# Pair loop of a hybrid RWKV-7 layer: the first inversion level made per direction, one PE item and the adaLN products moved

## The reference, cut to what matters

```
def step(S, inp):
    r_t, w_t, k_t, v_t, kk_t, b_t = inp
    sa = einsum('bhij,bhj->bhi', S, kk_t)
    S = S * w_t[:, :, None, :] - sa[..., None] * b_t[:, :, None, :] \
        + v_t[..., None] * k_t[:, :, None, :]
    return S, einsum('bhij,bhj->bhi', S, r_t)
# per direction d: first over the context, then over the latents from that state
mod = silu(c) @ w_mod + b_mod      # adaLN rows; (2048,) @ (2048, 12288)
```

## Time and profile before

| | |
|---|---|
| median of 3 runs | 2997.85 us (2994.82 to 2999.31) |
| the profiled execution's own time | 2995.07 us |
| its span in the profile | 2993.1 us |
| PE busy | 2841.4 us (95%) |
| DVE busy | 1839.5 us (61%) |
| ACT, POOL busy | 1002.5 us (33%), 579.6 us (19%) |
| mean DMA rate | 138 GB/s |
| mean granted TensorE clock | 0.979 |

### The profile page before, as it was taken

One profiled execution on the slowest core, in us unless ns is written; L12 is line 12 of the kernel. 1 busy time (PEld: TensorE's weight loads), 2 busy tenths in 40 slices (PEclk: granted clock), 3 DMA queues, 4 the chain that ended last, 5 costly groups with the idle time before them and its releaser, 6 DMA issues.

```text
span 2993.1 us, 70020 instructions
## 1 busy us (share of the span) xinstructions
PE 2841.4 (95%) x27808; PEld 2207.5 (74%) x27808; DVE 1839.5 (61%) x3324; ACT 1002.5 (33%) x1715; POOL 579.6 (19%) x708
## 2 busy tenths in 40 slices
PE   5899999999999999999989999999989999999997
PEld 1246665566656566666556699999979999999997
DVE  1115666677666767666675544444378888885434
ACT  1123322333322333332231433333354444443333
POOL 0003222333122233222231110000013333330000
PEclk9799999999999999999999999999989999999998
DMA  8621332222332222233214545554525555554553
GB/s 323 268 77 63 107 107 93 70 74 89 103 107 93 82 75 86 93 106 107 79 53 148 204 148 182 186 182 170 198 99 183 182 182 182 182 182 156 182 174 134
DMA packets 75291, 412.28 MB, mean 138 GB/s; under 512 B 9200, under 2 KB 11888, under 8 KB 42736
## 3 DMA queue, kind: packets, MB, share of 16 engines
q1 hardware_dynamic: 74352, 407.51, 39.5%
q0 software_dynamic: 768, 2.10, 0.2%
HBM read 405.38 MB, written 4.19 MB: 137 GB/s over the span
## 4 chain that ended last, share of the span: by engine, by line
PE 84%; DVE 8%; issue 3%; DMA 3%; ACT 1%; SPq 0%; DVEq 0%; ACTq 0%; PEldq 0%
PE PB L671 18%; PE Q L919 6%; PE Q L920 6%; PE Q L924 6%; PE PB L919 4%; PE PB L920 4%; PE PB L924 4%; PE CH L924 3%; PE CH L920 3%; PE CH L919 3%; DMA ring<-w_mod_dram 3%; PE Q L808 3%; PE PB L656 2%; PE Q L794 2%; PE Q L815 2%
## 5 line engine op out<-in xcount | busy, mean ns | idle before, releaser
L671 PE MATMUL PB<-hT,ring 128*128 128x512 f32 (+1 forms) x1536 | 673.5, 552 | 6.4 <-PEq L660 5.4
L1615 DVE TENSOR_TENSOR w_lo_r<-ring,w_hi_r 128x1536 fp32r<-128x1536 f32 (+3 forms) x178 | 386.9, 2174 | 269.8 <-ACT w_hi_r L1217 269.8
L1217 ACT ACTIVATE w_hi_r<-ring 128x2048 fp32r<-128x2048 f32 (+2 forms) x178 | 325.8, 1831 | 453.7 <-PE Q L924 211.3
L671 PEld LDWEIGHTS PB<-hT,ring 128*128 128x128 f32 x1536 | 256.8, 189 | 120.9 <-issue 70.7
L920 PE MATMUL PB<-hT_r,w_hi_r 128*128 128x256 f32 x832 | 204.6, 285 | 0.0
L1475 DVE SCALAR_TENSOR_TENSOR arena<-ring,csilp,arena 128x512 f32<-128x512 f32 x240 | 193.5, 806 | 5.2 <-DMA ring<-w_mod_dram 1.0
L1775 DVE TENSOR_TENSOR w_lo_r<-ring,w_hi_r 128x1408 fp32r<-128x1408 f32 x62 | 101.2, 1633 | 147.9 <-ACT w_hi_r L1331 147.9
L1876 POOL TENSOR_TENSOR w_lo_r<-ring,w_hi_r 128x512 fp32r<-128x512 f32 x88 | 118.4, 1346 | 361.4 <-ACT w_hi_r L1217 361.4
L919 PE MATMUL PB<-hT_r,w_hi_r 128*128 128x256 f32 x704 | 175.7, 289 | 4.7 <-DVE hT_r L1702 4.7
L919 PE MATMUL Q<-ff_hi_r,w_hi_r 128*128 128x256 f32 x704 | 175.6, 288 | 1.8 <-ACT w_hi_r L1331 1.8
L920 PE MATMUL Q<-ff_lo_r,w_hi_r 128*128 128x256 f32 x704 | 172.9, 284 | 0.0
(11 more groups left out here) (266 smaller groups left out, 6096.5 us busy)
## 6 DMA issues: line engine op xcount, KB each, us to landing
ring<-w_up_dram SPq DMA_DIRECT2D x88, 1024.0 KB, 4.8
ring<-w_mod_dram SPq DMA_DIRECT2D x128, 512.0 KB, 3.7
ring<-w_rkv_dram SPq DMA_DIRECT2D x48, 1024.0 KB, 5.8
ring<-w_down_dram SPq DMA_DIRECT2D x64, 704.0 KB, 4.0
ring<-w_mod_dram SPq DMA_DIRECT2D x32, 1024.0 KB, 7.8
ring<-w_ga_dram SPq DMA_DIRECT2D x16, 1024.0 KB, 4.8
ring<-w_gb_dram SPq DMA_DIRECT2D x16, 1024.0 KB, 4.8
ring<-w_pa_dram SPq DMA_DIRECT2D x16, 1024.0 KB, 4.8
```

The lines of the kernel that those rows point to most:

```text
L671: last = mm(PB[slot % 2][:, 0:cols], tile(n, kt), hT[:, kt, 0:cols], start=(kt == 0), stop=(kt == KT - 1))
L1217: f(w_hi_r[:, r % 2, 0:n], ring[:, r, 0:n], ACT.Copy).then_inc(hi_rdy, 1)
L1615: tt(w_lo_r[:, r, 0:n], ring[:, r, 0:n], as_f32(w_hi_r[:, r % 2, 0:n]), ALU.subtract).then_inc(lo_rdy, 1)
```

## The change

Four edits inside the pair loop:

- DVE makes the first level per direction: after the scores of d come TU (two operations of 64x256) and ZU (128x256) of d, and after NL of d come TL and ZL of d. Five operations of 512 columns become ten of 256. The signals `zu_rdy` and `zl_rdy` are still given once, behind d = 1.
- PE's first item (W0) goes ahead of the five waits that stand before the levels.
- The products move back: k = 0 to level 4, none in scan step 0, two in steps 1 to 6 (k = 2s-1, 2s), k = 13 in step 7, k = 14 and 15 behind the sum of the readout. Before, step s had k = 2s and 2s+1 and only k = 15 stood behind the sum.
- BODY_STEPS, the count of DVE's own semaphore steps in a pair, goes from 38 to 41.

```diff
@@ PE, body
+                if more >= 1:
+                    between(i + 1, 0)
+                else:
+                    behind_last(0)
                 pe.wait_ge(xt_sb, i * 4 + 4)
                 pe.wait_ge(nl_sb, i * 2 + 2)
                 pe.wait_ge(bonv_rdy, i + 1)
...
                 for lv in range(LEVELS - 1):
                     b = 2 << lv
-                    if lv == 0:
-                        if more >= 1:
-                            between(i + 1, 0)
-                        else:
-                            behind_last(0)
                     pe.wait_ge(zu_rdy, i * LEVELS + lv + 1)
@@ DVE, body, in the loop over d
+                    dve.wait_ge(sc_sb, i * 4 + 2 * d + 2)
+                    for h in range(2):
+                        hr = slice(64 - 64 * h, 128 - 64 * h)
+                        m = V.tick(tt(single(TU[hr], 1 - d), single(SC[d][h][hr, :, 0], 1 - d),
+                                      single(wide(off_mask[:, 0, 0, :], NCH)[hr], 1 - d), ALU.mult))
+                    V.need(m)
+                    z = tt(single(ZU[d], 1 - d), single(wide(eye2[:, :], NCH), 1 - d), single(TU, 1 - d), ALU.subtract)
                     if d == 1:
-                        dve.wait_ge(sc_sb, i * 4 + 4)
-                        for h in range(2):
-                            hr = slice(64 - 64 * h, 128 - 64 * h)
-                            m = V.tick(tt(by_chunk(plain(TU[hr], 1)), woven(SC2[h][hr, :, :, 0], 1),
-                                          plain(wide(off_mask[:, 0, 0, :], NCH)[hr], 1), ALU.mult))
-                        V.need(m)
-                        tt(by_chunk(woven(ZU2, 1)), plain(wide(eye2[:, :], NCH), 1), by_chunk(plain(TU, 1)), ALU.subtract).then_inc(zu_rdy, 1)
+                        z.then_inc(zu_rdy, 1)
                     dve.wait_ge(nl_ps, i * 2 + d + 1)
                     tt(NL[d], chunks(Q[0][:, :]), wide(score_mask[:, 1 - d, 0:C], NCH), ALU.mult).then_inc(nl_sb, 1)
-                dve.wait_ge(nl_sb, i * 2 + 2)
-                flow(tt(by_chunk(plain(TL, 1)), by_chunk(woven(NL2, 1)), plain(wide(off_mask[:, 0, 0, :], NCH), 1), ALU.mult))
-                tt(by_chunk(woven(ZL2, 1)), plain(wide(eye2[:, :], NCH), 1), by_chunk(plain(TL, 1)),
-                   ALU.subtract).then_inc(zl_rdy, 1)
+                    dve.wait_ge(nl_sb, i * 2 + d + 1)
+                    flow(tt(single(TL, d), single(NL[d], d), single(wide(off_mask[:, 0, 0, :], NCH), d), ALU.mult))
+                    z = tt(single(ZL[d], d), single(wide(eye2[:, :], NCH), d), single(TL, d), ALU.subtract)
+                    if d == 1:
+                        z.then_inc(zl_rdy, 1)
@@ DVE, levels
                         for n in range(2 * lv + (lv == 0), 2 * lv + 2):
                             inputs(i + 1, n)
+                        if lv == LEVELS - 2:
+                            mod_product(i, 0)
@@ DVE, scan
                     if more >= 1:
-                        for k in range(2 * s, min(2 * s + 2, 15)):
+                        for k in range(max(2 * s - 1, 1), min(2 * s + 1, 14)):
                             mod_product(i, k)
...
                 tt(ra, yd[0], yd[1], ALU.add).then_inc(ysum_rdy, 1)
                 if more >= 1:
+                    mod_product(i, 14)
                     mod_product(i, 15)
```

More of the change, by code:

```diff
@@ L34 @@
 QUAD = P // 4
-BODY_STEPS = 38
+BODY_STEPS = 41
 ARENA = 32100
@@ L448, in plain, with single @@
             return bass.AP(v.tensor, v.offset, walk([part] + chunk, col, b, b))
+        def single(v, odd):
+            return v.rearrange("p c (n two) -> p c n two", two=2)[:, :, :, odd]
         def by_chunk(v):
```

## The result

The changed kernel takes 2962.61 us in the median of 4 runs (2958.76 to 2965.55), the kernel before 2998.44 (2994.82 to 2999.31) beside it. The profiled execution took 2960.52 us, 34.55 less than that of before; the prediction's sum had 28.8.

The account below looks back on a forecast made before the run. PE bounds the kernel, waiting 41.6 us, mostly behind a late DVE. Levels 16.5, scan 13.6, pair 14 1.5, readout -2.8 sum to 28.8 us off: 2969 us against 2997.85, range 2958 to 2987.

Parts of the forecast that it names:

- What bounds: Pair loop: PE is busy nearly always; its waits in four totals, 41.6 us, are the most the change can give.
- Levels, 1.10 a pair: Start of the levels: half operations at 0.42 to 0.55 us close PE's gaps of 0.60 and 0.51; 16.5 us in 15 pairs.
- rival 4: Levels: the shift is swallowed by something seen as hidden, POOL's copy or a bank held by ACT; 2977 us, chance 0.13.
- The item: Start of the levels: W0, no longer waiting for NL, starts at 709.61, which saves 0.60 us.
- Level 4, 0.25: Product k = 0 waits for a POOL operation, so the last ZU update starts 0.25 us late; bounds 0 and 1.5.
- Scan, 0.97 a pair: Scan step 1: waits of 0.42 and 0.90 go, less 0.25 for level 4 and 0.1 left; 13.6 us in 14 pairs.
- Rival 1: Scan step 1: all of the 0.90 stays because the L1545s meet POOL operations; 2982 us, or 2988; chance 0.17.
- Pair 14 and the ends: Pair 14, with no second projection beside its scan, waits more; 1.5 us taken for it.
- Readout, 0.2: Two products behind the sum make L1571 0.3 us late; PE loses 0.2 a pair, -2.8 us in 14 pairs.
- Loads, nothing: Half loads in the scan: issue to need falls to 4.4 us against a median landing of 3.7; hidden, 0.7 to spare.
- Rival 2: Levels: half operations cost like whole ones, 4 us slower, 3002 us; chance 0.05.

Follow-up runs that it names:

- the table early: The changed kernel with ACT loading the tanh table ahead of its wait for the projections, not ahead of W0's tanh: 2958.61 us, ratio 0.9872.
- the experiment: The changed kernel with each half load (2 to 7) asked for one product later, computation the same: 2984.12 us, ratio 0.9952.

## Why the prediction was right, and where it was off

- **What bounds.** Right: four waits of PE behind DVE, 41.6 us, of which 33.6 are gone, and behind the loop nothing changes.
- **Levels, 1.10 a pair.** Measured 1.18, 0.93 ahead of L797 and 0.25 up to L811. The half operations cost 0.43 to 0.58 for the second direction where 0.42 to 0.55 was taken, up to 0.85 for the first, and those lie in DVE's idle time. The total is close because two misses cancel: a removed wait gave 0.33 more than its row, and part of **rival 4** is true, since ACT's table load holds W0's bank. "Everything behind it on PE shifts by this, as ACT's work is not in the way" was wrong, by about 0.3 a pair: so much the period falls with the table early.
- **The item.** "The item W0 no longer waits for NL ... which saves the 0.60" puts the saving on the wrong edit. The item alone gives 1.0003, and the half operations without it all of the gain: NL is early enough for either order.
- **Level 4, 0.25.** The mechanism was right, the price too high: the product took 1.49 for its 0.91, but PE lost 0.12. The product ended 0.28 behind the POOL operation, as the sum had it, but the ZU update started only 0.17 later against PE's list, and not 0.25. Those 0.12 are what the product in step 0 wins back (0.11).
- **Scan, 0.97 a pair.** This is the term that was mis-sized: it measured 1.40, so 19.6 us in 14 pairs where the sum has 13.6. Nothing is left of the 0.90 (0.1 was kept), level 4 cost 0.13 less, and the last 0.2 are again what a wait costs beyond its row: from slices to slices the two stretches with the waits took 1.95 and 2.43 (744.91, 746.86, 749.29) and now take 1.44 and 1.43 (731.92, 733.36, 734.79), 1.51 less for 1.32. Rival 1, that the port keeps the 0.90, is out: with the levels alone that wait is still 14.0 us, with the products alone 1.7. But one step of the working was wrong as well: the pair was to meet two POOL operations once more and end near 747.3, two microseconds behind the copy. It met one and took 0.74. Why it met two before and now one, no run shows.
- **Pair 14 and the ends.** Pair 14 gave 1.7 us, where the sum has 1.5 for its scan and 1.1 for its levels.
- **Readout, 0.2.** 0.28.
- **Loads, nothing.** Right, 1.5 us of DVE's waits in all. The "0.7 to spare" was near as well: with one product (0.74) less of it 33 of 84 loads were late. The late loads cost 0.5 us a pair there, and the larger part of the experiment's loss lies in pairs 14 and 15.
- **Rival 2**, half operations as dear as whole ones, is out by their rows.

The Trainium skill's rule of a fixed extra cost for each operation in SBUF ("VectorE: DVE Perf Modes", "The TRN2 errata — SBUF-src ops pay a fixed extra latency per instruction") gives an estimate of 424 ns for a half, and the trace agrees (0.43, with every second column). It did not decide here, because the whole operations that they replace took 0.81 to 1.16 and not the 0.69 of the rule.

That a removed wait gives back more than its row (0.93 for 0.60 at the levels) is read from starts in two traces; the one wait that was removed by itself, that for the SSQ bank, gave 0.41 a pair for 0.33. What stays open is why the loop starts up to 7 us later in some profiled executions (253.53 to 260.31 us), and POOL's part in the scan's waits, since no run changes POOL's operations.

## What to carry to other kernels

When the bounding engine waits for another that is not full, ask what stands ahead of the late operation in that engine's queue and how much of it needs only half of the inputs: splitting work by direction moved it into idle time, and that, not a new order on the waiting engine, made the gain. A reordering on the waiting engine alone moves the gap to the next wait on the same late producer. And before work is moved later, compare request-to-need with the landing time of each load: here one product of 0.74 us made 33 of 84 loads late. The same shift cost 0.5 us a pair where DVE had slack behind the late product, and 9.1 us in the one pair where four products stood ahead of an update that PE waits for.

## What the runs showed of the hardware

- The products and the small scaling operations of DVE, which read SBUF, ended 0.2 to 0.3 us behind the GpSimd operation that they met: the product k = 0 took 1.49 us beside POOL's L1810, 0.93 in step 0 and 0.48 at level 0 with POOL idle; a product with two SBUF operands 1.75 for 0.74. The ZU update, whose second input is in PSUM, took 0.67 beside L1809. This agrees with the Trainium skill, "SBUF — State Buffer", section "Who interferes with whom", by which a two-port mode, or a second SBUF input beside a GpSimd operation that reads SBUF, makes one of the two wait for a whole instruction. What I had not expected is how little of it reaches PE, 0.12 and 0.26 us.
- A table load on ACT (as the Trainium skill has it, 1283 ns in "ScalarE activation tables: per-element evaluation and per-set limits", section "What a function is on this engine") took 1.28 us and was on PE's path through a bank that it kept full. Ahead of an idle wait it cost nothing that the trace shows.
- With PE idle for 4.03 and 1.97 us in two steps, the granted clock was 0.71 in the mean of 16 us, after 1.00 in the 40 us in which PE was busy nearly throughout. Behind the gaps two slices took 2.07 us for 1.12, and the kernel took 3326 us for an expected 3240 to 3280.
- The 512 KB loads land in 3.4 to 7.0 us with a median of 3.7, and with 3.85 us between request and need DVE waited for 33 of 84 loads in the full pairs, with 4.59 us for none of them. The median alone would have called both hidden.
